# Two transformer blocks on one core: row sums of the mLSTM's weights moved from TensorE to VectorE, a zeroing moved from the output product into the mLSTM, and routing and experts joined in one program

## The reference

```python
# mLSTM of one head, written over all pairs of time steps t >= s
s = einsum('td,sd->ts', q, k) * exp(b_t - b_s + log_i_s - m_t)
num = einsum('ts,sv->tv', s, v)
den = sum(s, axis=-1)
h = num / maximum(abs(den), exp(-m_t))
...
# experts: each token's two blocks' outputs are added into its row of y
y = zeros((T, D)).at[slot_tok].add(out.reshape(cap, D))
```

## Time and profile before

| | |
|---|---|
| median of 3 runs | 3573.45 us (3573.07 to 3573.51) |
| profiled execution | 3573.72 us, span of its instructions 3572.0 us |
| mean granted clock of TensorE | 0.937 |
| busy: PE, DVE, ACT, POOL | 3073.5, 1613.8, 1364.6, 778.5 us |
| mlstm, from its first PE product to the last DVE write | 2296.1 to 2704.6 us |
| gm, go | to 2890.4, to 3005.4 us |
| norm_route, experts with the last norm | from 3009.1, from 3073.7 us |

### The profile page before, as it was taken

The page is one execution under the profiler, slowest core; times in us unless marked ns, Lnnn a source line. Parts: engine busy times, 40 slices in busy tenths (PEclk is TensorE's granted clock), DMA queues, the critical chain, the costliest instruction groups (busy, mean ns, idle before and its releaser), DMA issues. The chain is left out here.

```text
span 3572.0 us, 41010 instructions
## 1 busy us (share of the span) xinstructions
PE 3073.5 (86%) x14663; PEld 2446.1 (68%) x14663; DVE 1613.8 (45%) x2481; ACT 1364.6 (38%) x2009; POOL 778.5 (22%) x389
## 2 busy tenths in 40 slices
PE   6999977699877999674998989899998969799994
PEld 4777756488756877453666668777776856688883
DVE  6443467433453334523322231133334123799997
ACT  3333331444224432222333332122212113689995
POOL 1111001244323443110000002212211211244341
PEclk8999988799988999887999999999999989899997
DMA  5000042233522326210000012210101232578774
GB/s 208 31 18 6 1 171 112 65 100 94 177 94 82 100 78 210 107 41 22 15 15 7 7 42 70 78 37 34 47 23 59 75 114 108 193 257 274 269 257 147
DMA packets 83334, 343.20 MB, mean 96 GB/s; under 512 B 21045, under 2 KB 27477, under 8 KB 72225
## 3 DMA queue, kind: packets, MB, share of 16 engines
q1 hardware_dynamic: 63000, 316.64, 25.4%
q0 software_dynamic: 17856, 16.85, 2.2%
q10 hardware_dynamic: 2376, 8.46, 0.7%
HBM read 375.84 MB, written 45.69 MB: 118 GB/s over the span
## 5 line engine op out<-in xcount | busy, mean ns | idle before, releaser
L2461 DVE TENSOR_TENSOR ex_g_lo<-ex_g_raw,ex_g_hi 128x1024 fp32r<-128x1024 f32 x188 | 221.1, 1218 | 0.7 <-ACT ex_g_hi L2401 0.5
L2401 ACT CAST ex_g_hi<-ex_g_raw 128x1024 fp32r<-128x1024 f32 x188 | 191.8, 1052 | 14.7 <-PEq L1918 13.4
L618 DVE TENSOR_TENSOR ff_gated<-psum,ff_silu 128x512 f32<-128x512 f32 x44 | 30.4, 692 | 313.6 <-PE psum L490 313.6
L490 PE MATMUL psum<-ff_h_hi,ff0i_w_hi 128*128 128x512 f32 x352 | 137.9, 392 | 23.3 <-POOLq L443 23.3
L490 PE MATMUL psum<-ff_h_hi,ff1i_w_hi 128*128 128x512 f32 x352 | 138.0, 392 | 23.0 <-POOLq L443 23.0
L446 POOL TENSOR_TENSOR ff0i_w_lo<-ff0i_w_raw,ff0i_w_hi 128x1024 fp32r<-128x1024 f32 x43 | 106.4, 2473 | 211.9 <-ACT ff0i_w_hi L414 211.9
L2344 PE MATMUL psum<-ex_g_hi,ex_x_hi 128*128 128x512 f32 x376 | 150.8, 401 | 0.0
L977 ACT ACTIVATE ba_probs<-ba_logits,ba_stats 128x385 f32<-128x385 f32 (+1 forms) x128 | 75.6, 590 | 193.5 <-DVE ba_stats L1022 193.1
L446 POOL TENSOR_TENSOR ff1i_w_lo<-ff1i_w_raw,ff1i_w_hi 128x1024 fp32r<-128x1024 f32 x43 | 106.3, 2473 | 188.3 <-ACT ff1i_w_hi L414 188.3
L2345 PE MATMUL psum<-ex_g_lo,ex_x_hi 128*128 128x512 f32 x376 | 146.9, 391 | 0.0
L2346 PE MATMUL psum<-ex_g_hi,ex_x_lo 128*128 128x512 f32 x376 | 146.8, 391 | 0.0
(11 more groups left out here) (543 smaller groups left out, 8504.9 us busy)
## 6 DMA issues: line engine op xcount, KB each, us to landing
ex_g_raw<-in_w_experts_gu_dram SPq DMA_DIRECT2D x32, 2048.0 KB, 7.8
ex_d_raw<-in_w_experts_d_dram SPq DMA_DIRECT2D x32, 1024.0 KB, 9.9
ff0i_w_raw<-in_ffn_in_dram SPq DMA_DIRECT2D x44, 512.0 KB, 3.6
ff1i_w_raw<-in_ffn_in_dram SPq DMA_DIRECT2D x44, 512.0 KB, 3.6
wom_w<-in_mod_w_dram SPq DMA_DIRECT2D x8, 2048.0 KB, 8.0
ff0o_w_raw<-in_ffn_out_dram SPq DMA_DIRECT2D x16, 704.0 KB, 4.4
ff1o_w_raw<-in_ffn_out_dram SPq DMA_DIRECT2D x16, 704.0 KB, 4.2
ga_w_raw<-in_w_merge_a_dram SPq DMA_DIRECT2D x16, 512.0 KB, 3.6
```

What stands on the lines that cost most here:

```text
L490: mm = nc.tensor.matmul(chip.psum[:, 2 * u + h, :], w[:, v % 2, k * P:(k + 1) * P], (a[u] if isinstance(a, tuple) else a)[:, c * n_kc + k, ...
L2401: nc.scalar.copy(cols(g_hi, n), cols(raw.g_raw[i % 3], n)).then_inc(q["g_hi_made"], 1)
L2461: nc.vector.tensor_tensor(cols(g_lo, n), cols(raw.g_raw[i % 3], n), cols(g_hi, n).bitcast(F32), ALU.subtract).then_inc(q["g_lo_made"], 1)
```

## The change

It does three things.

1. **Sums on VectorE.** The product with `chip.ones` in every unit goes. DVE keeps `wsum`, a 128 x 512 tile for each half: a copy of `wt` for the half's first unit, an addition for each other one, each right behind the multiplication that made `wt`. After the last unit of a half PE makes one product of 512 columns of `wsum` with `chip.ones` into the bank that held the sums.
2. **Zeroing in the mlstm.** POOL's memset and SP's four DMAs move out of `gated_output`. The memset becomes the first instruction of POOL in `mlstm`, and the DMAs stand at the end of SP's stream there, behind the last head's last weight tile. SP then waits for them before the block ends.
3. **One program.** `experts` becomes `experts_programs`, five functions that `norm_route` calls at the ends of its five streams. The barrier and the drain between them go. In its place PE waits until ACT has copied the last tile out of PSUM, DVE until the token-major rows are stored, and SP until `token_ids` are made. Otherwise the instructions of both are the same, in the same order.

```diff
@@ mlstm @@
+    wsum = chip.place("ml_wsum", [P, 2, HALF], F32, X_AT)
+    zero = chip.place("ml_zero", [P, D // 4], F32, C_AT + 3 * KIB)
...
         def _(sp):
...
+            sp.wait_ge(s_["zero_made"], 1)
+            for c in range(4):
+                sp.dma_start(sums_dram[:, c * (D // 4):(c + 1) * (D // 4)].rearrange("(i p) d -> p i d", p=P),
+                             zero[:].rearrange("p (o d) -> p o d", o=1).broadcast_to([P, NB, D // 4])).then_inc(s_["zeroed"], 16)
+            sp.wait_ge(s_["zeroed"], 64)
...
         def _(pool):
+            nc.gpsimd.memset(zero[:], 0.0).then_inc(s_["zero_made"], 1)
...
             def floor_den(h, c):
                 dve.wait_ge(s_["applied"], NU * h + (4, NU)[c])
+                dve.wait_ge(s_["totalled"], 2 * h + c + 1)
...
                     if u >= 2:
                         dve.wait_ge(s_["applied"], NU * h + u - 1)
+                        dve.wait_ge(s_["added"], NU * h + u - 1)
                     nc.vector.scalar_tensor_tensor(wt[:, u % 2, 0:w], chip.psum[:, u % 2, 0:w], 0.25 * P ** -0.5,
                                                    ew[:, u % 2, 0:w], ALU.mult, ALU.mult).then_inc(s_["weighted"], 1)
+                    dve.wait_ge(s_["weighted"], NU * h + u + 2)
+                    if j == 0:
+                        nc.vector.tensor_copy(wsum[:, c, :], wt[:, u % 2, :]).then_inc(s_["added"], 1)
+                    else:
+                        dve.wait_ge(s_["added"], NU * h + u)
+                        nc.vector.tensor_tensor(wsum[:, c, t0:t0 + w], wsum[:, c, t0:t0 + w], wt[:, u % 2, 0:w],
+                                                ALU.add).then_inc(s_["added"], 1)
...
                         pe.wait_ge(s_["weighted"], NU * h + x + 2)
-                        for i in range(XV + 1):
-                            lhs = v[:, j, i * P:(i + 1) * P] if i < XV else chip.ones[:]
-                            mm = nc.tensor.matmul(chip.psum[:, 2 + 3 * c + i, t0:t0 + w], lhs, wt[:, x % 2, 0:w],
-                                                  start=(j == 0), stop=(j == 4 * c + 3))
+                        for i in range(XV):
+                            mm = nc.tensor.matmul(chip.psum[:, 2 + 3 * c + i, t0:t0 + w], v[:, j, i * P:(i + 1) * P],
+                                                  wt[:, x % 2, 0:w], start=(j == 0), stop=(j == 4 * c + 3))
                         mm.then_inc(s_["applied"], 1)
+                        if j == 4 * c + 3:
+                            pe.wait_ge(s_["added"], NU * h + x + 1)
+                            nc.tensor.matmul(chip.psum[:, 2 + 3 * c + XV, :], chip.ones[:], wsum[:, c, :],
+                                             start=True, stop=True).then_inc(s_["totalled"], 1)
@@ gated_output: the zero tile, its memset, start_sp's four DMAs and end_sp's wait go @@
@@ norm_route, at the end of the streams @@
+            go_on["sp"](sp, q)
+            go_on["pool"](pool)
+            go_on["pe"](pe, q)
+            go_on["act"](act)
+            go_on["dve"](dve, t_stored)
@@ experts -> experts_programs @@
+    def on_sp(sp, route):
+        sp.wait_ge(route["ids"], 2)
         combine.start_sp(sp)
...
+    def on_pe(pe, route):
+        pe.wait_ge(route["copied"], 2 * NB)
...
+    def on_dve(dve, t_stored):
+        for u in range(2):
+            dve.wait_ge(t_stored[u], 16 * NB // 2)
...
+    return {"sp": on_sp, "pool": on_pool, "pe": on_pe, "act": on_act, "dve": on_dve}
```

More of the change, by code:

```diff
@@ L1801, in start_sp @@
             sp.sem_inc(x_in[u], 16)
[L1802 to L1811, removed]
     def on_sp(sp, j, u):
@@ new lines, in on_sp, with on_pool, gather, store @@
+    def on_sp(sp, route):
+        sp.wait_ge(route["ids"], 2)
+        combine.start_sp(sp)
+        for i in range(3, N_BLK + 1):
+            if i < N_BLK and order[i] < NE:
+                g_free(sp, i)
+                raw.load_g(sp, i, order[i])
+            if i >= 4 and order[i - 1] < NE:
+                d_free(sp, i - 1)
+                raw.load_d(sp, i - 1, order[i - 1])
+        combine.on_sp(sp)
+    def on_pool(pool):
+        def gather(i):
+            pool.wait_ge(q["x_turned"], i - 2)
+            raw.gather(nc.gpsimd, i, xg, h_tm_dram, token_ids)
+        def store(i):
+            pool.wait_ge(q["o_made"], i + 1)
+            if i >= 1:
+                pool.wait_ge(stored[1 - i % 2], 16 * ((i + 1) // 2))
+            nc.gpsimd.indirect_dma_start(out=sums_dram[:, :],
+                                         out_offset=bass.IndirectOffsetOnAxis(ap=token_ids[:, order[i]:order[i] + 1], axis=0),
+                                         in_=o[:, i % 2, :], in_offset=None, bounds_check=S - 1, oob_is_err=False,
+                                         compute_op=ALU.add).then_inc(stored[i % 2], 16)
+        for i in range(N_BLK):
+            if i + 3 <= LAST:
+                gather(i + 3)
+            if i + 3 <= LAST and order[i + 3] >= NE:
+                g_free(pool, i + 3)
+                n = order[i + 3] - NE
+                raw.load_more_g(nc.gpsimd, i + 3, more_rows[:, n:n + 1])
+            if i + 2 <= LAST and order[i + 2] >= NE:
+                d_free(pool, i + 2)
+                n = order[i + 2] - NE
+                raw.load_more_d(nc.gpsimd, i + 2, more_rows[:, n:n + 1])
+            if i >= 1:
+                store(i - 1)
+        store(LAST)
+        pool.wait_ge(stored[0], 16 * ((N_BLK + 1) // 2))
+        pool.wait_ge(stored[1], 16 * (N_BLK // 2))
+        pool.sem_inc(combine.ready, 1)
@@ new lines, in on_act, with split_g, split_d, split_x @@
+    def on_act(act):
+        def split_g(i, n):
+            if n == 0:
+                raw.wait_in(act, i, raw.g_in, raw.more_g_in)
+            if i >= 1:
+                act.wait_ge(q["g_used"], GC * (i - 1) + n + 1)
+            nc.scalar.copy(cols(g_hi, n), cols(raw.g_raw[i % 3], n)).then_inc(q["g_hi_made"], 1)
+        def split_d(i, n):
+            if n == 0:
+                raw.wait_in(act, i, raw.d_in, raw.more_d_in)
+            if i >= 1:
+                act.wait_ge(q["d_used"], DC * (i - 1) + n + 1)
+            nc.scalar.copy(cols(d_hi, n), cols(raw.d_raw[i % 3], n)).then_inc(q["d_hi_made"], 1)
+        def split_x(i):
+            act.wait_ge(q["x_turned"], i + 1)
+            if i >= 2:
+                act.wait_ge(q["g_used"], GC * (i - 1))
+            nc.scalar.copy(flat(x_hi, i), psum_x).then_inc(q["x_hi_made"], 1)
+        def split_a(i):
+            act.wait_ge(q["a_turned"], i + 1)
+            if i >= 2:
+                act.wait_ge(q["d_used"], DC * (i - 1))
+            nc.scalar.copy(a_hi[:, i % 2, :], psum_a(i)).then_inc(q["a_hi_made"], 1)
+        def silu(i):
+            act.wait_ge(q["g_used"], GC * i + GC)
+            if i >= 1:
+                act.wait_ge(q["a_made"], i)
+            nc.scalar.activation(sil[:], chip.psum[:, i % 2, 0:DE], ACT.Silu).then_inc(q["silu_made"], 1)
+        def copy_out(i):
+            act.wait_ge(q["d_used"], DC * i + DC)
+            if i >= 2:
+                act.wait_ge(stored[i % 2], 16 * (i // 2))
+            nc.scalar.copy(o[:, i % 2, :], psum_o).then_inc(q["o_made"], 1)
+        for n in range(GC):
+            split_g(0, n)
+        split_x(0)
+        for i in range(N_BLK):
+            more = i < LAST
+            if i >= 1:
+                split_a(i - 1)
+                split_d(i - 1, 1)
+            if more:
+                split_x(i + 1)
+                for n in range(GC - 1):
+                    split_g(i + 1, n)
+            silu(i)
+            if more:
+                split_g(i + 1, GC - 1)
+            split_d(i, 0)
+            if i >= 1:
+                copy_out(i - 1)
+        split_a(LAST)
+        split_d(LAST, 1)
+        copy_out(LAST)
+        combine.on_act(act)
@@ L2644, in two_blocks @@
               beside=GateRows(chip, lat[:, 0, :], A["gate_bias"], decay_rows, g_cols))
-        mlstm(chip, A["w_ml"], A["w_mlv"], A["conv"], decay_rows, g_cols, h[0], h[1], branch)
+        mlstm(chip, A["w_ml"], A["w_mlv"], A["conv"], decay_rows, g_cols, h[0], h[1], branch, sums)
         merged = chip.place("merged", [P, KD, S], F32, X_AT)
@@ L2650, in two_blocks @@
         squares = gated_output(chip, A["w_out"], merged_s[0], merged_s[1], 64, x_mid,
-                     halves=Halves(chip, "me_s", merged, merged_s[0], merged_s[1], KD), sums_dram=sums)
+                     halves=Halves(chip, "me_s", merged, merged_s[0], merged_s[1], KD))
         chip.renew_semaphores()
```

331 lines of the change are left out of this document (113 added, 218 removed).

## The result

| | before | changed |
|---|---|---|
| runs shown with the result | 3572.68 to 3573.51 us, median 3573.26 (4) | 3536.19 to 3541.81 us, median 3540.42 (4) |
| ratio | | 0.9906, 95% interval 0.9889 to 0.9924 |
| profiled execution | 3573.72 us, span 3572.0 | 3540.87 us, span 3538.9 |

The account below looks back on a forecast made before the run. PE was taken to bound the unit loops, a DMA the start of go, POOL's drain the expert border. 12.0 + 2.5 + 2.5 = 17.0 us less than 3573.7 gave 3556.7 us; eight-in-ten range 3538.5 to 3561.5.

Parts of the forecast that it names:

- the choice in the tie: Unit 6, three heads: POOL's long split gets the ports before DVE's addition, PE idles 5.0 us; chance 0.58.
- The walk: Step through a head's twelve units with traced durations; put the old loop at 31.4 us against 31.6 measured.
- a row whose DVE instruction isn't of the addition's kind: Trace row before the change: DVE 0.04 us ahead of POOL was itself held for 3.67 us.
- Sums in the DVE-wins case: Unit loops: POOL waits 0.6 us and the loops save 3 x 4.5 + 4.9 = 18.4 us.
- Zeroing: Start of go: first weight cast 4.4 us after the last write instead of 16.4; 12.0 us less.
- Border: Routing to experts: PE waits for one gather instead of POOL's drain of three; 2.5 us less.
- The first rival: DVE wins the tie at unit 6, in all or some heads; 3540.8 us if it wins; chance 0.30.
- The forecast case: POOL wins the tie at unit 6 in three heads; 17.0 us less in all, 3556.7 us; chance 0.58.
- The clock: Unit loops after PE's idle time: half speed for at most 3.4 us, taken as 1.2 us lost per head.
- the clock stays down: Rival: low clock lasts through the loop into the next head's projections; 18.5 us per head gives 3580.9; chance 0.04.
- The zeroing's place: Zeros' DMAs start in the last head's projections, near 2630, costed at nothing under other work.
- the bounds: Part 1, the sums: 6.1 us less (no clock loss) to 0.5 less (2 us in each head).

Follow-up runs that it names:

- The run with the third operand: Changed kernel with unit 6's addition written as multiplication by a column of ones plus addition; 3558.8 us, ratio 0.9954.
- 0.1 us of delay: Changed kernel with one more, already fulfilled semaphore wait of DVE ahead of unit 6's addition; 3559.1 us, ratio 0.9958.
- the three kernels with such idle times: Changed kernel with a column operand in unit 6's addition (3558.8 us), a fulfilled wait before it (3559.1), or ScalarE's v cast one unit sooner (3552.0).
- both kernels that lost the tie: Changed kernel with a column operand in unit 6's addition (3558.8 us), or with a fulfilled wait of DVE ahead of it (3559.1 us).

## Why the prediction was wrong

- **The step that failed is the choice in the tie**: "So I take POOL to win." The walk had put DVE 0.01 us ahead, and that was right to a hundredth of a microsecond; I overruled it with a row whose DVE instruction isn't of the addition's kind. With such an instruction in the addition's place POOL does win. Of the rule of the Trainium skill that the prediction weighed against it ("SBUF — State Buffer", section "Who interferes with whom": whoever issues first has the ports for its whole length) the letter was right for the addition. The run with the third operand says that the recorded start isn't always the moment that counts.
- **The rest of the sum held.** Sums in the DVE-wins case: 18.4 forecast, 18.8 in the loops. Zeroing: 12.0 forecast, 11.8. Border: 2.5 forecast, 2.0; the first gather took 0.9 us longer on POOL, which the sum had at nothing. The first rival's 3540.8 us stands against 3540.4 measured, with 0.30 of chance given to it where 0.58 went to the other side. That the two lie within 0.4 us is in part luck: the stretches that the sum doesn't name moved by up to 2.6 us each and cancel.
- **The forecast case exists.** With 0.1 us of delay the kernel takes 3559.1 us beside 3575.5 of the kernel before, 16.4 less for 17.0 forecast. The total is nearer than its parts: the four loops save 1.2 us there (127.0 to 125.8) where the sum had 2.5. In them: PE idle 4.73 us for 5.0 said, a loop of 31.3 us without the clock's loss for 31.0. The clock was mis-sized: I took 1.2 us for a head, which fits the head where PE worked 3.4 us at half speed (1.1), but not those with 4.3 and 6.1 us (1.6 and 2.4). I had one row of 3.4 us and took it for the length it always has.
- **The rival "the clock stays down"** would have needed 6.9 us of loss in a head; the largest in the three kernels with such idle times was 2.6.
- **The zeroing's place** was wrong by 38 us, near 2592 and not 2630, at no price, since cover was there on both sides. That the cover is what makes it free was right; uncovered it cost 12.4 us.
- A slip in the bounds: 2 us of clock loss in each of three heads would leave 4.9 - 3 x 1.6 = 0.1 us of part 1, not 0.5.
- Range and direction held. With a tie to 0.02 us and 17.5 us behind it, the evidence that I used could not choose. The row that would have helped was a DVE instruction with two tiles and no column starting within 0.1 us ahead of POOL. The trace of before has none beside one of POOL's splits.

## What to carry to other kernels

When a sum hangs on which of two engines gets a shared resource first, price both sides, and treat the kernel as unstable even if it comes out well: one fulfilled wait, 0.1 us, cost 17.5 us in the loops here, and the cure is to move the long instruction to where nobody needs the resource, not to tune the lead. Before a row is used to settle such a tie, look whether it has the same operands. And an instruction that is long but needs one port only can be the cover of something: shorten it after what it covers has been moved.

## What was not expected of the hardware

- The tie at unit 6 went the same way in every head of a kernel. The lead of 0.012 to 0.014 us repeated in fifteen heads of five profiles and on both chips, and each time the plain addition had the ports first; with nearly the same lead (0.011 or 0.012) the one with a column had them second in all three heads.
- TensorE's clock after the same idle time differs from head to head. 3.1 us of idle were followed by half the clock for 6.8 us, not at all, and for 3.4 us in three heads of one execution, and 4.73 us by 6.8, 6.8 and 3.4 us in both kernels that lost the tie.
- An increment that POOL's program has behind an indirect DMA can come before that DMA's own work on POOL has begun (3023.70 for 3023.94).
- POOL's gather at the border ended 2.32 us after the start of DVE's two-tile split in eleven profiles, whatever its own start.
